# A decoder step with a two-level mixture of experts: another order for GpSimd's gathers and scatters in the expert loop

## What is computed

```python
h = rmsnorm(x); proj = h @ w_in
x = x + concat(pool_mixer(...), gla_mixer(...)) @ w_out
x = x + hier_moe(rmsnorm(x), ...)     # top group of 4, then top 2 of its 4 experts
y = rmsnorm(x, final_g)
# one expert, over the tokens that chose it, with weight c:
acc += c * ((silu(x @ w_gate) * (x @ w_up)) @ w_down)
```

## Time and profile before

| | |
|---|---|
| median of 3 runs | 1047.48 us (1046.59 to 1048.64) |
| the profiled execution's own time | 1046.07 us |
| its span, first to last instruction | 1043.9 us |
| TensorE busy, share of the span | 943.8 us, 90% |
| VectorE / ScalarE / GpSimd busy | 459.8 / 308.8 / 199.1 us |
| expert loop, first z to last z (16 rounds) | 563.0 to 1026.4 us |
| mean granted TensorE clock | 0.953 of full speed |

### The profile page before, as it was taken

The page is one execution under the profiler, slowest core; times in us unless marked ns, Lnnn a source line. Parts: engine busy times, 40 slices in busy tenths (PEclk is TensorE's granted clock), DMA queues, the critical chain, the costliest instruction groups (busy, mean ns, idle before and its releaser), DMA issues. The chain is left out here.

```text
span 1043.9 us, 15883 instructions
## 1 busy us (share of the span) xinstructions
PE 943.8 (90%) x5943; PEld 817.1 (78%) x5943; DVE 459.8 (44%) x1164; ACT 308.8 (30%) x625; POOL 199.1 (19%) x247
## 2 busy tenths in 40 slices
PE   5988999999999889999179999999999999999983
PEld 3568766766776568888169999999999999999983
DVE  4418533345673553642734333344333444433332
ACT  4556233333444232643002212222221222221121
POOL 1000000000000000000031344433334433324441
PEclk9998998999999889999579999999999999999997
DMA  8311023101010190733028887687897777799740
GB/s 266 115 41 41 1 53 69 41 1 41 1 41 1 46 314 8 242 145 118 25 65 276 291 276 251 234 277 241 287 306 246 260 248 243 251 316 294 252 154 20
DMA packets 126883, 167.02 MB, mean 160 GB/s; under 512 B 14996, under 2 KB 98040, under 8 KB 126853
## 3 DMA queue, kind: packets, MB, share of 16 engines
q1 hardware_dynamic: 111493, 136.03, 39.9%
q0 software_dynamic: 15360, 30.59, 8.2%
HBM read 147.39 MB, written 41.17 MB: 181 GB/s over the span
## 5 line engine op out<-in xcount | busy, mean ns | idle before, releaser
L1602 PE MATMUL bank<-xT,ring 128*128 128x160 f32 x2048 | 287.0, 301 | 1.0 <-DVE xT L1778 1.0
L1602 PEld LDWEIGHTS bank<-xT,ring 128*128 128x128 f32 x2048 | 280.5, 191 | 3.7 <-issue 3.7
L1614 PE MATMUL bank<-hid,wdn 128*128 128x160 f32 x1024 | 151.2, 301 | 14.4 <-DVE hid L1786 11.2
L419 PE MATMUL bank<-hT,ring 128*128 128x384 f32 (+1 forms) x480 | 160.0, 489 | 0.0
L1614 PEld LDWEIGHTS bank<-hid,wdn 128*128 128x128 f32 x1024 | 141.3, 190 | 18.2 <-DVE hid L1786 14.5
L419 PEld LDWEIGHTS bank<-hT,ring 128*128 128x128 f32 x480 | 94.4, 199 | 57.5 <-issue 11.2
L1690 ACT ACTIVATE sg<-bank 128x160 f32<-128x160 f32 x64 | 19.5, 305 | 230.9 <-PE bank L1602 220.3
L1524 POOL DMA_INDIRECT out<-ot,lists_out x64 | 84.0, 1312 | 19.8 <-issue 19.8
L1786 DVE TENSOR_TENSOR hid<-sg,bank 128x160 f32<-128x160 f32 x64 | 20.5, 320 | 134.1 <-ACT sg L1690 124.8
L1803 DVE COPY yT<-bank 128x256 f32<-128x256 f32 x32 | 13.6, 425 | 123.0 <-PE bank L1614 123.0
L1535 POOL TENSOR_TENSOR hold_at<-ident 128x1 f32<-128x1 f32 x47 | 11.8, 251 | 271.8 <-DVE ot L1825 233.7
(11 more groups left out here) (310 smaller groups left out, 1354.5 us busy)
## 6 DMA issues: line engine op xcount, KB each, us to landing
wdn<-in_w_down SPq DMA_DIRECT2D x32, 1024.0 KB, 8.3
ring<-in_w_gate SPq DMA_DIRECT2D x32, 1024.0 KB, 6.3
ring<-in_w_up SPq DMA_DIRECT2D x32, 1024.0 KB, 10.3
x<-in_x_prompt SPq DMA_DIRECT2D x16, 512.0 KB, 7.0
ring<-in_w_in SPq DMA_DIRECT2D x8, 1024.0 KB, 9.0
ring<-in_w_out SPq DMA_DIRECT2D x4, 1024.0 KB, 5.0
h_rows<-h SPq DMA_DIRECT2D x8, 512.0 KB, 2.6
sums<-x SPq DMA_DIRECT2D x8, 512.0 KB, 3.6
```

The costliest lines, as they stand in the source:

```text
L419: mm = nc.tensor.matmul(acc(n)[:, 0:tn], ring[:, u % 4, k, c0:c0 + P], hT[:, k, t0:t0 + tn], start=k == 0, stop=k == KC - 1)
L1602: x = nc.tensor.matmul(bank[f % 2][:, side * 256:side * 256 + W], ring[:, u, k, c0:c0 + P], xT[:, k, :], start=k == 0, stop=k == KC - 1)
L1614: x = nc.tensor.matmul(bank[2 + j % 2][:, q * 256:q * 256 + W], wdn[:, d // 4, k * 512 + (d % 4) * P:k * 512 + (d % 4 + 1) * P], hid[:, k, ...
```

## The change

In the loop, GpSimd's first `hold()` no longer waits for the normalised rows (`e_ot`). The four result scatters, which stood between the scatter of the sums and the gather of the next rows, now stand behind that gather, and the wait for `e_ot` stands at the second `hold()`. No instruction is added or dropped, apart from how waits are laid on register instructions.

```diff
@@ -1553,15 +1553,15 @@
             pool.wait_ge(e_hold, i * 3 + 3)
             pool.wait_ge(e_last, i + 1)
             pool.wait_ge(e_z, i * 3 + 4)
-            pool.wait_ge(e_ot, i * 2 + 2)
             hold()
             send(1, sums_dram, N, z, z2, e_out)
-            send_results(e_out)
             pool.wait_ge(e_hold, i * 3 + 4)
             pool.wait_ge(e_idx, i + 3)
             pool.wait_ge(e_xt, i * 3 + 6)
+            pool.wait_ge(e_ot, i * 2 + 2)
             hold()
             rows_x()
+            send_results(e_out)
             pool.wait_ge(e_out, i * 96 + 96)
             pool.sem_inc(e_free, 1)
             pool.wait_ge(e_hold, i * 3 + 5)
```

## The result

| | before | changed |
|---|---|---|
| median of the paired runs | 1047.03 us | 1054.97 us (1052.79 to 1055.89) |
| ratio, 95% interval | | 1.0072 (1.0050 to 1.0093) |
| the profiled execution | 1046.07 us, span 1043.9 | 1052.79 us, span 1050.7 |

The changed kernel is slower by 0.7%, 7.9 us. The page of after, group by group: busy time, mean ns, then idle time ahead and what ended it.

A forecast was written before the change was run, and what follows sets the result against it. TensorE was taken as the bound, 30.74 us a round. The profiled 1046.07 us + 0 for steps 1 to 4 + 0 for steps 5 and 6 gave 1046.1, forecast as a median of about 1047.4 us, range 1045.8 to 1058.

The forecast's parts named there:

- Steps 1 to 4: GpSimd: sums' scatters 4.49 us earlier, second hold 2.48 us, `xg` 4.9 earlier, last result scatter 2.90 later; TensorE cost 0.
- Step 5: From last result scatter to `old`: second `old` gather issued 1.2 to 2.9 us later than before.
- Step 6: Landing of `old`: served when a weight load ends, so about as before; cost 0, other end 1.67 us.
- 1.75 us of margin: In the round shown, `old` may land about 1.75 us later before TensorE waits; some rounds spare up to 1 less.
- the first step: Reading of the expert loop's chain of waits: TensorE almost alone bounds it, at 30.74 us a round.
- the ring: GpSimd's once-a-round chain from `z` through holds, scatters and gathers to the next `z`; 1.23 us to spare at `z`.
- Rival C: Faster, needing a TensorE wait on `xg` or on GpSimd's scatters in the loop; 1044 to 1045 us, chance 0.05.
- rivals A and B: A: the ring binds, 1059 or 1069 us, chance 0.20; B: only full rounds miss the load's end, 1050 to 1056, 0.12.

The follow-up runs named there:

- e3: The changed kernel with a 0.7 us GpSimd memset between the `xg` gathers and the result scatters: 1070.34 us.
- e4: The kernel before with a 0.7 us GpSimd memset between the hold and the `xg` gathers: 1067.01 us.
- e2: Against the kernel before, only the first half (sums early): sums scattered at once, results after their own wait for `ot`, `xg` still behind them: 1032.81 us.
- e15: The changed kernel without the third result scatter in the loop, the fourth in its old place behind pausing memsets: 1049.56 us.
- e1: Only the second half of the change: `xg` gathered ahead of the results, first hold still waiting for `ot` as in the kernel before: 1054.17 us.
- e14: The changed kernel without the two sample scatters in the loop, plus two memsets and an unread extra gather where the fourth scatter was: 1038.37 us.
- e17: The changed kernel with a one-column memset between the `xg` gathers and the result scatters: 1053.98 us.
- e13: The changed kernel without the two scatters of the sample rows in the loop: 1033.72 us.

## Why the prediction was wrong

- **Steps 1 to 4 held.** First scatter of the sums 753.54 − 750.75 = 2.79 us behind `z` (forecast 2.8); hold 2.45 us (2.48); fourth result scatter 768.87 − 750.75 = 18.12 (18.1), at 0.99 us. The rule of the Trainium skill on the exclusive lock ("SBUF — State Buffer", section "SBUF: two separate sides") agrees with the hold's 2.45 us. TensorE doesn't wait for the hold in any row.
- **Step 5 held**: second `old` gather 774.91 − 750.75 = 24.16 us behind `z`, at the early end of the 24.2 to 25.9 forecast; before 23.01.
- **Step 6 was right in its cost and mostly wrong in its mechanism.** Forecast was a landing at about 29.5 us as before, 4 to 6 us from issue. The tile `old` in after:

```profile
DMA to landing us min/median/max: 3.6/6.7/7.3
```

 before 4.0, 7.0, 7.5. Counted over the landings in the trace, the last one comes 27.8 to 29.9 us behind `z` in before and 29.4 to 31.1 in after (without the last round): on the mean about 1.2 us later, for issues 1.5 us later. So the landing did go later with the issue. Part of it is the 0.5 us by which the loads too come later in the round, since SyncE gets the same late signal; "which the change doesn't touch" was not so. It stayed inside the 1.75 us of margin, so the 0 us for this step held: no `z` waited. The edge was near all the same, as e3 shows. For `xg`, e4 shows a delay that grows: issued 0.7 us later it landed at 24.7 to 26.0 us behind `z`, before at 21.4 to 23.6. This would fit a turn that comes as a load ends; but in e4 the loads also start some 0.9 us earlier, so it isn't shown by itself. Turns packet by packet, as "DMA: Bandwidth & Descriptors", section "Queues, rings and completion order" of the Trainium skill has them, would hardly give 3 us for 0.7.
- **What failed is the first step, the reading of what bounds the kernel**: "the chain is made of matmuls, with gaps of some tenths of a microsecond", a round "is thus 30.74 us", and from it "+ 0 for steps 1 to 4, which lie beside TensorE's 29.82 us". One of those gaps, 0.87 us ahead of `down`, stood in the wait table with 14.4 us in all, as a wait for `hid`. I took it as part of the matmuls' time. It was a stall that depends on GpSimd's order, a way to reach TensorE without touching the ring: it measured +0.52 us in the round shown, 6.6 us in the whole loop, against my 0. Taking it away gave a round of 29.81 us (e2).
- **Rival C, "faster", was thrown out for the same cause**: "the chain shows none in the loop". Half of the change (e2) is a gain of 1.3% on the chip where before has the stall.
- **The range held the time by luck.** It reached up to 1058 us for the sake of rivals A and B; 1054.97 us lies in it by another cause than either.
- **Rivals A and B did not happen, and the stall probably hid them.** With a round of 31.27 us the ring has time. With the signal on time (e15, one of the two sample scatters left out) and the fourth scatter where it stands in after, `z` waits up to 3.3 us and the time is 1049.56 us. So mending the late signal alone would hardly have made the changed order good.

**What stays open** is why the signal is late. Shown: it comes with `xg` ahead of the results (e1) and not with early sums (e2), but for that kernel's last round; one issue at that moment doesn't bring it (e14, e15, beside a late control), nor does the fourth scatter as such (e15); with a pause of 0.7 us ahead of the last two issues it is gone from before (e4), and a memset that makes no pause leaves it (e17). In after and in before with the stall, in all 15 rounds, the slice's end falls on an issue that is at least the sixth in an unbroken run, to 0.04 us. The third slice's end falls about 0.6 us into the fifth in a row of before's and is never late. That the number of back-to-back issues decides, together with the place of the last, is argued from these, not shown by a run of its own. It can't be the whole rule either: the second slice's signal, which costs nothing as TensorE doesn't wait for it, came about 0.75 us late in 9 of 15 rounds of before, during the third issue in a row (the one that meets the one-hot instruction). For before the late signal was there in some groups of runs and not in others, for after in all three that ran it. As each group is one chip at one time, that the chip is what differs isn't shown. Not tried were a break that pauses without moving the later issues, and before with its `xg` gathers moved by a tenth of a microsecond.

The version to keep is "sums early": 1032.81 and 1031.49 us on two chips, faster than both kernels there.

## What to carry to other kernels

Before a round's length is taken as the busiest engine's own time, add up what that engine waits in the loop and name each wait, even those of under 1 us: here 14.4 us stood in the table, and one half of the change removed them while the other half raised them to 21. Then split a reordering into its halves and time each: one half alone gave −13.3 us, the other +8.0, and both together +7.9, so the halves don't add up and the net tells nothing of either. And a signal that comes late to an idle neighbour is a cost of its own. It is read as the time from the end of the work to the neighbour's start, and a second engine that waits for the same signal tells whether the signal or the neighbour is late.

## What the runs showed of the hardware

- A signal of TensorE's reached an idle ScalarE 0.98 us late in before and 1.50 us late in after, and SyncE as late. With GpSimd's issues fewer (e13), paused (e4) or ended 2.6 us ahead (e2, but for its last round) the same signal, that of the fourth slice, came within 0.1 us.
- The same kernel took 1031.5, 1033.9, 1035.0, 1046.1, 1046.5 and 1047.0 us in six groups of runs. On the chip with 1033.9 its wait ahead of `down` was 0.7 + 0.7 us instead of 11.2 + 3.2. The changed kernel took 1052.2 to 1055.0 us in the three groups that ran it.
- A wait of TensorE of under 2 us can cost more than itself. In e3 the 112 matmuls of a round's slices behind a wait for the squares, and the windows around (the clock is third from the end):

```profile
758.64 0.38 PE L1635 MATMUL bank<-ssq,same 128*128 128x1 f32 x2 [1.79 <-ACT squares L1703]
...
758.89 17.13 PE L1604 MATMUL bank<-xT,ring 128*128 128x160 f32 x112
```
```profile
754.44:758.64 4.20, 2.42 (x17) 2.17 (x16) 1.87 (x4) 1.81 (x7) 0.19 (x1) 1.00 0.72 258
758.64:776.06 17.42, 17.42 (x116) 17.42 (x117) 7.51 (x25) 3.89 (x8) 10.53 (x10) 0.90 0.47 158
```

 In after the same 112 take 15.46 us at a clock of 1.00. Here TensorE had been busy 2.42 of 4.20 us, and the mean granted clock of the next 17.42 us was 0.90 (full speed is the 2.4 GHz level): 1.67 us lost on top of the wait. This came in 4 rounds of e3, behind waits of 1.66 to 2.37 us; ten others with waits of 1.23 to 2.02 us kept their 15.46 us, so the wait's length alone doesn't tell. The stalls of 0.87 and 1.39 us at `down` showed no such fall.
